# Gated sum of two expert rows as diagonal fp32 products on TensorE in the tail of a streaming encoder step

## What is computed

```
gates = p_grp * (top_p / sum(top_p))              # two gates per token
y = zeros.at[buf_tok].add(yb * buf_gate[:, None])  # per token: gate0 * row0 + gate1 * row1
x = x + y                                          # residual
y_out = x * rsqrt(mean(x * x) + EPS) * norm_f_g    # last RMSNorm
```

## Time and profile before

| | us |
|---|---|
| median of 3 timed runs (1126.06 to 1126.88) | 1126.14 |
| the profiled execution | 1123.9 |
| its span, first to last instruction | 1122.2 |
| last scatter issued | 1073.91 |
| first multiply-add of the tail | 1082.04 |
| last final multiplication starts | 1117.48 |

### The profile page before, as it was taken

How to read it: one execution, slowest core, us unless ns; L and a number is a source line. 1 busy time by engine, 2 the same in 40 slices (tenths; PEclk the granted TensorE clock), 3 DMA queues, 4 the chain that set the end, 5 groups by cost and what they waited for, 6 DMA issues and landing times. The chain is left out here.

```text
span 1122.2 us, 13663 instructions
## 1 busy us (share of the span) xinstructions
PE 932.8 (83%) x4446; PEld 768.6 (68%) x4446; DVE 949.6 (85%) x964; ACT 614.8 (55%) x597; POOL 370.6 (33%) x300
## 2 busy tenths in 40 slices
PE   4997977278469999469999999999999999999620
PEld 3786766255346887458888888888888888888510
DVE  6289999999987687859999898988989889898548
ACT  7213412116343322247778787887878778787323
POOL 2138969636662110312223122222222223221100
PEclk8998988689589999589999999999999999999865
DMA  8201100103004132468999999999999999998756
GB/s 254 95 20 37 38 19 19 56 1 116 4 19 150 58 119 87 175 266 320 404 380 391 398 377 402 392 400 392 384 396 372 393 382 381 395 376 346 274 241 246
DMA packets 66587, 268.63 MB, mean 239 GB/s; under 512 B 15503, under 2 KB 28303, under 8 KB 40889
## 3 DMA queue, kind: packets, MB, share of 16 engines
q1 hardware_dynamic: 56761, 250.36, 58.6%
q0 software_dynamic: 9792, 17.85, 4.1%
HBM read 254.61 MB, written 31.38 MB: 255 GB/s over the span
## 5 line engine op out<-in xcount | busy, mean ns | idle before, releaser
L1352 DVE TENSOR_TENSOR big<-arena,big 128x2048 fp32r<-128x2048 f32 x128 | 287.1, 2284 | 0.0
L692 ACT ACTIVATE big<-arena 128x2048 fp32r<-128x2048 f32 x128 | 237.6, 1908 | 0.0
L1110 DVE SCALAR_TENSOR_TENSOR arena<-arena,cols 128x512 f32<-128x512 f32 (+2 forms) x210 | 226.4, 1133 | 1.9
L982 PE MATMUL ps<-big,ring 128*128 128x512 f32 x512 | 203.6, 398 | 2.4 <-DVE ring L1357 2.4
L983 PE MATMUL ps<-big,ring 128*128 128x512 f32 x512 | 200.7, 392 | 0.0
L984 PE MATMUL ps<-big,ring 128*128 128x512 f32 x512 | 200.7, 392 | 0.0
L768 PE MATMUL ps<-big,ring 128*128 128x512 f32 (+2 forms) x432 | 164.6, 381 | 40.8 <-DVE ring L1175 16.5
L769 PE MATMUL ps<-big,ring 128*128 128x512 f32 (+2 forms) x432 | 162.8, 377 | 0.0
L770 PE MATMUL ps<-big,ring 128*128 128x512 f32 (+2 forms) x432 | 161.4, 374 | 0.0
L1352 DVE TENSOR_TENSOR slot_tail<-arena,slot_tail 128x2048 fp32r<-128x2048 f32 x64 | 143.5, 2283 | 1.1 <-ACT slot_tail L692 1.1
L768 PEld LDWEIGHTS ps<-big,ring 128*128 128x128 f32 (+1 forms) x432 | 83.9, 194 | 56.6 <-issue 25.8
(11 more groups left out here) (215 smaller groups left out, 1338.1 us busy)
## 6 DMA issues: line engine op xcount, KB each, us to landing
arena<-in_w_eg SPq DMA_DIRECT2D x64, 1024.0 KB, 8.0
arena<-in_w_eu SPq DMA_DIRECT2D x64, 1024.0 KB, 9.1
arena<-in_w_ed SPq DMA_DIRECT2D x64, 1024.0 KB, 9.5
arena<-in_x_prompt SPq DMA_DIRECT2D x16, 512.0 KB, 5.0
arena<-y_scratch SPq DMA_DIRECT2D x8, 1024.0 KB, 12.6
arena<-in_w_in SPq DMA_DIRECT2D x12, 512.0 KB, 3.7
arena<-in_w_out SPq DMA_DIRECT2D x8, 512.0 KB, 3.6
x_scratch<-arena SPq DMA_DIRECT2D x8, 512.0 KB, 2.6
```

The source lines that it names most:

```text
L692: act.activation(we_h[n % SLOTS], raw[n % RAWS], ACT.Copy).then_inc(high_done, 1)
L982: pe.matmul(out, part_h[b][:, k, :], wh[:, i, :], start=(k == 0), stop=False)
L1110: dve.scalar_tensor_tensor(hc[:, c, a:b], v_ext[:, c, a + j:b + j], cols[:, c, j:j + 1], hc[:, c, a:b], ALU.mult, ALU.add).then_inc(conv_s ...
L1352: dve.tensor_tensor(we_l[n % SLOTS], raw[n % RAWS], we_h[n % SLOTS].bitcast(F32), ALU.subtract).then_inc(low_done, 1)
```

## The change

For each tile, ScalarE writes two 128x128 diagonal matrices, the identity scaled row by row with one of the two gates (`gate_diagonals`). They lie in `act_t`, two sets for two tiles in flight. TensorE multiplies them with the token's two rows and sums in PSUM, four products of 512 columns per tile (`weighted_sum`). VectorE adds the PSUM tile to the residual in one instruction. The diagonals of tiles 0 and 1 are made ahead of the tail's loop, those of tile t + 2 after the square root of tile t. SyncE's loads of tiles 6, 7 and 8 wait for TensorE's new semaphore `f_mix`.

```diff
+        diag = act_t.rearrange("p (s k n) -> p s k n", s=2, k=2)
...
                 if t + FB < NT:
-                    sp.wait_ge(f_acc, 2 * t + 2)
+                    sp.wait_ge(f_mix, t + 1)
                     load_y2(t + FB)
...
+            def gate_diagonals(t):
+                r = ROWS[t]
+                if t >= 2:
+                    act.wait_ge(f_mix, t - 1)
+                for k in range(2):
+                    act.activation(diag[0:r, t % 2, k, 0:r], ident[0:r, 0:r], ACT.Copy,
+                                   scale=gates[0:r, k, t:t + 1]).then_inc(f_diag, 1)
+
+            act.wait_ge(act_done, 2 * n_pairs + 2)
+            gate_diagonals(0)
+            gate_diagonals(1)
             for t in range(NT):
                 r = ROWS[t]
-                act.wait_ge(f_acc, 2 * t + 2)
+                act.wait_ge(f_acc, t + 1)
...
                                scale=1.0 / D).then_inc(f_sd, 1)
+                if t + 2 < NT:
+                    gate_diagonals(t + 2)
...
+            def weighted_sum(t):
+                r, s = ROWS[t], t % FB
+                pe.wait_ge(f_in[s], 16 * (t // FB + 1))
+                pe.wait_ge(f_diag, 2 * t + 2)
+                if t >= 2:
+                    pe.wait_ge(f_acc, t - 1)
+                for k in range(2):
+                    for c0 in (0, BANK):
+                        ins = pe.matmul(out_ps[t % 2][0:r, c0:c0 + BANK], diag[0:r, t % 2, k, 0:r],
+                                        y_in[s][0:r, k * D + c0:k * D + c0 + BANK], start=(k == 0), stop=(k == 1))
+                ins.then_inc(f_mix, 1)
+
+            pe.wait_ge(ye_done, 2 * n_pairs + 2)
+            for t in range(NT):
+                weighted_sum(t)
...
             def combine(t):
-                r, s = ROWS[t], t % FB
+                r = ROWS[t]
                 dve.wait_ge(f_x[t], 16)
-                dve.wait_ge(f_in[s], 16 * (t // FB + 1))
-                for k in range(2):
-                    dve.scalar_tensor_tensor(x_in[t][0:r, :], y_in[s][0:r, k * D:(k + 1) * D], gates[0:r, k, t:t + 1],
-                                             x_in[t][0:r, :], ALU.mult, ALU.add).then_inc(f_acc, 1)
-                    dve.wait_ge(f_acc, 2 * t + k + 1)
+                dve.wait_ge(f_mix, t + 1)
+                dve.tensor_tensor(x_in[t][0:r, :], out_ps[t % 2][0:r, :], x_in[t][0:r, :], ALU.add).then_inc(f_acc, 1)
```

More of the change, by code:

```diff
@@ L270, in trunk_kernel @@
         f_out = sem("f_out")
+        f_diag, f_mix = sem("f_diag"), sem("f_mix")
         prod_done, help_done, win_done, scaled_done, wl_dve = map(sem, (
```

## The result

The changed kernel takes 1128.89 us as the median of 20 runs, against 1126.45 us for the kernel before in 20 runs of its own: a ratio of 1.0023 with a 95% interval of 1.0013 to 1.0032, 2.4 us more. 1129.4 had been predicted, in a range from 1127.0 to 1131.4. The profiled execution took 1128.11 us, its span 1126.1.

A forecast was written before the change was run, and what follows sets the result against it. VectorE's own queue was taken as the bound. First sum with low clock, table-load wait, then three two-tile loops of 7.16 us end the last addition at 1119.09 against 1115.76: +3.3 on 1126.14, 1129.4 us, range 1127.0 to 1131.4.

The forecast's parts named there:

- TensorE's pace: Tail, gated sums on TensorE: eight fp32 records per tile, 0.43 us from start to start, 3.44 us a tile.
- The loop over ScalarE: Tail, from sum t to sum t+2 through addition, Square, Sqrt and diagonals: 7.16 us for two tiles, 3.58 per tile.
- The table load: Tail, tile 0's first Sqrt loads its table, so TensorE waits 1.5 us for tile 2's diagonals.
- The low clock at the start: Tail's first products run at 1.2 GHz after TensorE's idleness: 2.2 us lost, bounds 1.9 and 3.4.
- TensorE's pace alone (the first): Rival, tail: TensorE's product time rules and the diagonals hide; +2.5 or +2.2 us, 1128.5; chance 16%.
- The cheap sum (the second): Rival, tail: sums cost less than line 863's rows, VectorE's 2.75 us is the pace; -5 us, 1121; chance 9%.
- The third: Rival, tail: TensorE's clock stays at or falls back to 1.2 GHz; +29 us, or about +13 if half; chance 5%.
- Late transfers (the fourth): Rival, tail: the last load lands 0.8 us after it is wanted; +4.1 us, 1130.2; chance 5%.

## Why the prediction was right

The sum had four terms that the trace can be held against.

- TensorE's pace, 3.44 a tile and 0.43 a record from line 863: 3.43 in the run with all diagonals ahead. Right, and with half the work the tail fell by 8.2 us, so that this was the term that decides.
- The loop over ScalarE, 7.16 for two tiles: 7.20 measured. Its parts held too: the pair of diagonals, taken as 0.67 from copies of another width, is 0.68, and the addition 1.22. Only for tile 8 was it shorter: its diagonals are 64 wide, and the sum of three tiles from 1107.67 on shows no wait.
- The table load, a wait of 1.5 ahead of tile 2: 1.37, and 1.23 us of the tail gone when the load was moved. The trace put this wait down to "issue", not to ScalarE's diagonals as I had written; it took ScalarE's rows, where the diagonals end 0.09 us ahead of the product, and the experiments to name it. By the Trainium skill, "ScalarE: Activation LUTs", section "What ACT_TABLE_LOAD costs", a drain of about 1380 ns comes on top of the load. In the kernel after the load runs from 1091.00 to 1092.28 and the Sqrt starts at 1092.30; here too the trace shows no drain.
- The low clock at the start, 2.2 us with bounds of 1.9 and 3.4: this is the term that was mis-sized. It cost 1.4, because the clock came up after 2.7 us of products, sooner than in any of the three stretches that I had read (3.9, 5.3, 3.9). The lower bound was the shortest of three rows, and that is no bound.

With 1.4 for 2.2 the sum gives +2.5, and +2.6 was measured. So the mechanism held and one size was off by 0.8 us. The time came out closer than that, 0.5 us from the forecast, by luck: the kernel before stands at 1126.45 in its twenty runs and not at the 1126.14 of the three that I added to.

Of the rivals: TensorE's pace alone (the first) had priced the change at +2.2 to +2.5, as near to the measured 2.4 as the forecast's +3.3 or nearer, so the time does not tell the two apart. The trace does: TensorE's pace did not rule, since even tiles waited longer than odd ones and two tiles took 7.20 us and not 6.88, until the diagonals were moved. The cheap sum (the second) is refuted by 0.43 a record, though the side it named is real: at half the cost the kernel is faster by 0.6%. The third fell: the clock read 1.00 from 1086.2 to the end in spite of a wait at every second tile. The swing of the clock that "TensorE: Matmul & The Clock Gate" in the Trainium skill (section "A second HAM failure mode: psum-queue depth-cycling") reports of another kernel did not show here, with waits of 0.1 to 1.4 us. Late transfers (the fourth) were not seen in the kernel after; they came up only where the tail was 3 to 6 us shorter than before.

The probabilities put 72% on slower by more than 0.2%. The measured 0.23% lies just over that line, and its interval reaches down to 0.13%.

## What to carry to other kernels

In this kernel, moving work from a full engine to an idle one was worth only the difference between the full engine's old time and the idle engine's time per tile, here 4.03 - 3.44 = 0.6 us and not the 1.3 that VectorE saved, and the idle engine brought its own start: a low clock, operands that a third engine has to make, and everything that this third engine does in order ahead of them. Look for the same shape and type elsewhere in the trace before the move: line 863 had the price of a tile to a hundredth. If both engines can do the work, sharing it is worth a try. Here the split's tails, 32.7 to 33.9 us, are shorter than VectorE's alone (36.7) and TensorE's alone without its waits (35.7); timed, it is clear of the kernel before, while the intervals overlap with TensorE's alone (0.9975 to 0.9999).

## What was not expected

- The clock's rise is not a fixed price: the low stretch at the start of the tail was 2.7 us in the kernel after and some 3.5 in the run with half the work, against 3.9 to 5.3 read before, the first two of those at the same kind of work. In the shared kernel it read 1.00 for the first 3.9 us of idleness and was low by the end of 9.5 us.
- Runs of the same kernel spread over some 7 us (1122.41 to 1129.16 in the twenty of before), where the three that the prediction began from lay within 0.8. The profiled executions, one of each kernel, differ in when the tail begins, 1082.0 to 1086.6. Of the two furthest apart, the kernel before and the one with the early table load, the last scatters of result rows are issued at 1073.91 and 1078.47, 4.56 apart, and an early pair of the expert loop, at 561.84 and 566.04, is 4.20 apart already. So most of that difference had arisen by 562 us, in code that no edit touches; what causes it was not looked into.
